# Two transformer blocks on one core: joined slots in the paired-head attention stages, reordered stage ends, a multiplication with a second result, and two weight tiles split early

## The chip, the cores and the metric

The program runs on one core of one Trainium2 chip. The metric is the device time of one execution in microseconds (us), as the median of three runs. The core's engines are TensorE (PE in the profile, PEld for its weight loads), VectorE (DVE), ScalarE (ACT), GpSimd (POOL) and SyncE (SP, which here only issues DMAs). Each works through its own instructions in order and waits on semaphores that the others raise.

## What is computed

Two blocks of two layers each on a sequence of 512 tokens with 1024 features, all in float32. Cut to what matters here:

```python
def first_block(...):                       # two layers
    h = h + even_mixer(...)                 # layer 0: moba attention (8 heads), diff attention (4 x 2 heads)
    h = h + conv_ffn(...)                   # up, 3-tap convolution, gelu, product, down
    h = h + odd_mixer(...)                  # layer 1: dilated attention (8 heads), low-rank attention "mla" (4 heads)
    h = h + conv_ffn(...)
    return rmsnorm(h, final_norm)

def second_block(...):                      # two layers, each:
    ya = global_axial_attention(...)        # 8 query heads
    yb = pool_mixer(...)
    yc = neighbourhood_attention(...)       # 8 heads
    merged = jnp.sum(gates * z, axis=2)     # gated sum of the three branches
    mix = jnp.einsum('bsd,de->bse', merged, w_out[l])
    x = x + rmsnorm_2(mix, norm_mix_post[l])
    f = conv_gated_mlp(rmsnorm_2(x, norm_ffn_pre[l]), ...)
    x = x + rmsnorm_2(f, norm_ffn_post[l])
```

## The kernel before

**Matrices.** Activations lie transposed, 128 features x 512 tokens to a tile. Every float32 operand of a projection is held as a high and a low part (`hh`/`hl`, `yh`/`yl`, `acth`/`actl`, `mh`/`ml` for activations, `wh`/`wl` for weights), and `three` (L513 to L520) makes one product of 128 x 128 by 128 x 512 with three matmuls (L518, L519, L520). Such a trio is called a part below. An output tile of a 1024-deep projection takes eight parts. SP loads weight tiles (entries) into `raw[0]` and `raw[1]` by turns, POOL splits each with a cast (L474) and a subtraction (L476) into slot 0 or 1 of `wh` and `wl`, and may do so only when the product that read that slot before is done (`entry_done`). Results go to the PSUM banks PA, PB, S0, S1, T0, T1, O0, O1.

**Paired-head attention stages** are moba, dil, axial (twice) and na (twice). Each has 32 tiles of scores: four groups g of two heads, each with four query tiles. All engines run over the same slots t (`attention`, one function on each engine):

- PE, at even t: the scores of tiles t and t+1 (S0 and S1, L733; the two heads use 64 rows of the array each). At every t: as many waiting projection parts of the next group as the list `FILL` or the last plan says, then the transposes of tile t-3 (`transposed`, L646, into T0 or T1 by turns). At even t also the products with the values of the tile pair that ends with t-5 (`weighted_pair`, L781).
- DVE, at t: `score` moves the scores out of PSUM with the bias and the row minimum (L1679; axial L1675); at odd t `scale_pair` takes two reciprocals (L1690) and multiplies two tiles of exponentials by them in place (L1693).
- ACT, at t: the exponential of tile t (`soften_here`, L1338), and behind it the copy of the transposes of tile t-3 from T0 or T1 to SBUF (`copy_turned4`, L1343). In axial, ACT has the root for the next queries ahead of the exponential at t%8 = 6 (`q_root`, L1407).

The transposes of tile tt wait for `p_scaled` of tt (DVE) and for the ACT copy of tile tt-2, which held the same bank. The value products wait for the copies of both their tiles. `FILL` is 3, 3, 2, 2, 3, 3, 0, 0 parts for t%8 = 0 to 7 (axial 3, 3, 2, 0, 0, 0, 0, 0, with the rotation of the next queries, `q_turn`, at t%8 = 5). A pair is an even slot and the odd one behind it; the pair at t%8 = 6 has no parts in groups 0 to 2. It is called an empty pair.

**Other stages that the change touches.** diff is an attention stage with the same slots but one map per two tiles; DVE's `take_k` (L1749) frees PB and makes the next keys. mla runs four heads through 16 score tiles. At the ends of blocks `x_add` on DVE (L1927, L1929, L1582) and `renew_out` on ACT (L1287, L1290, L1291) add the residual, split the sum and make squares; with `early=True` (after diff, stage out0) the first four tiles lie in PA, PB, S1 and S0. In the second block out2 (`out_tiles`) is followed by a norm (`stat_last`), and by up2, whose first unit runs gate and value product side by side. `turning` (L571) is filler work on PE.

Of the kernel before, what the change touches and what calls it, by code (L numbers as in the profile page):

```python
# [11 lines left out]
S = 512  # L12
P = 128
# [20 lines left out]
    "na_v": (4, 1024), "na_qk": (6, 1024), "merge": (24, 1536), "out2": (8, 1024), "up2": (44, 1024), "down2": (16, 1536),  # L34
# [148 lines left out]
def build(nc, x_in, weights, consts, cols_in, lam_in, rel_in, rpb_in, strips_rel, strips_na, out):  # L183
    with ExitStack() as ctx:
# [159 lines left out]
        def flat(t):  # L344
# [5 lines left out]
                 (spare[:, :], yl[:, 8:10, :].rearrange("p a n -> p (a n)"))]  # L350

# [109 lines left out]
        def _(pool):  # L461
# [4 lines left out]
            def split(name, b):  # L466
                count, width = SEGMENTS[name]
                with pool.Fori(0, count // 2) as i:
# [31 lines left out]
            for n in SEG1:  # L500
                if n == "diff_v":
                    split_diff_v(here("diff_v"))
                else:
                    split(n, here(PHASE_OF.get(n, n)))
            for layer in range(LAYERS2):
                for n in SEG2:
                    split(n, here(PHASE_OF.get(n, n), layer))
# [3 lines left out]
        def _(pe):  # L511
# [186 lines left out]
            def attention(b, b0, kind, last_parts=(), last_plan=()):  # L698
# [43 lines left out]
                for t in range(end + 1):  # L742
# [6 lines left out]
                    for part in parts[max(sum(slots[:t]), begun):sum(slots[:t + 1])]:  # L749
                        part()  # L750
                    if kind == "diff":
                        if t % 2 == 0 and 0 <= t - 4 < 32:
                            difference_turn(b, (t - 4) // 2)
# [3 lines left out]
                    tt = t - T_BEHIND  # L757
                    if 0 <= tt < 32:
                        if tt < 2:
                            pe.wait_ge(v_copied, 4 * b["v"] - 1 + tt)  # L760
                        pe.wait_ge(p_scaled, b["ps"] + tt + 1)
                        pe.wait_ge(pt_copied, u + tt + 1)
                        transposed(tt, span(tt), maps4).then_inc(pt_ready, 1)
                    tv = t - V_BEHIND
                    if 0 <= tv < 32:
                        g, head = tv // 8, tv % 2
                        if head:
                            if tv == 1:
                                pe.wait_ge(y_split, 2 * b["g"] + 1)
                            if tv % 8 == 1:  # L770
                                pe.wait_ge(o_taken, u + 8 * max(g - 1, 0) + 2)
                            pe.wait_ge(pt_copied, u + tv + 3)
                            weighted_pair(OB[g % 2], tv // 2, span(tv), lambda head, k: values(g, 64 * head, k))
# [111 lines left out]
            def first_head(b):  # L885
# [5 lines left out]
                return [query, lambda: head_query(b, 0, False), lambda: head_key(b, 0), lambda: head_turn(b, 0), lambda: head_values(b, 0)]  # L891

            def mla(b, o):
# [26 lines left out]
                for t in range(16 + 3):  # L920
# [25 lines left out]
                    if 0 <= tv < 16:  # L946
                        if tv % 4 == 0:
# [4 lines left out]
                                 lambda k: head_v[tv // 4 % 2][:, k * P:k * P + P]).then_inc(o_ready, 1)  # L952
                out_part(o, 0, 2, (5, 7))
# [52 lines left out]

            def up(b, squared):
# [6 lines left out]
                if squared:  # L1014
                    pe.wait_ge(pa_taken, b["a"] + 1)
# [190 lines left out]
            def moba_stat():  # L1206
# [23 lines left out]
                      [1, 0, 0, 0, 1, 0, 0, 0, 1, 1, 1])  # L1230
# [4 lines left out]
            for l in range(LAYERS2):  # L1235
# [9 lines left out]
                out_tiles(H("out2", l), lambda k: (mh[:, k, :], ml[:, k, :]), m_split, H("out2", l)["m"], 1)  # L1245
# [9 lines left out]
        def _(act):  # L1255
# [24 lines left out]

            def renew_out(b, gain_at, early=False):

                def both(i, banks):
                    for j, (bank, taken) in enumerate(zip(banks, (pa_taken, pb_taken))):
                        n = 2 * i + j
                        act.wait_ge(xs_ready, b["xs"] + n + 1)
# [1059 lines left out]
```

## Time and profile before

| what | us |
|---|---|
| median of 3 runs | 3023.19 (3022.72 to 3024.15) |
| the profiled execution | 3022.8 |
| its span, first to last instruction | 3021.0 |
| PE busy in the span | 2975.2 |
| POOL busy | 1659.4 |
| DVE busy | 1449.0 |
| ACT busy | 774.2 |

A matmul's row lasts longer than its share of the engine, because matmuls overlap: the distance from one start to the next is what counts. An idle time in brackets behind a row is counted from the modelled end of the instruction before. The PEclk column of a stretch gives the share of TensorE's clock that was granted: 1.00 is 2.4 GHz, and 0.5 is 1.2 GHz.

### The profile page before, as it was taken

To read this page: it belongs to the slowest core of one execution; us is meant where nothing else is said; L and a number is where in the kernel's file an instruction comes from. 1 tells how busy PE (TensorE), PEld (TensorE's weight loads), DVE (VectorE), ACT (ScalarE), POOL (GpSimd) and SP (SyncE) were. 2 spreads that over 40 slices of the span, in tenths; PEclk is the share of its full clock that TensorE was granted. 3 is DMA by queue.
4 is the path that set the end of the run, shared out by engine and by line. 5 is a ranking of instruction groups with operands and counts; after the bars stand their busy time and mean duration, and the time that the engine had idled before them with its cause. 6 is when DMAs were issued, how large, how long until landed. Compare 5 with 4: busy or idle time off the path is not lost.

```text
span 3021.0 us, 41775 instructions
## 1 busy us (share of the span) xinstructions
PE 2975.2 (98%) x14292; PEld 2347.9 (78%) x14292; DVE 1449.0 (48%) x2511; ACT 774.2 (26%) x1419; POOL 1659.4 (55%) x1254
## 2 busy tenths in 40 slices
PE   8999999999999999999999999999999999999999
PEld 6767888887688888777688878888767788778887
DVE  4455444225544442365543476640575544576621
ACT  3343222113432210163411132210262411122200
POOL 4434666664156666533266656667423366556674
PEclk9999999999999999999999999999999999999999
DMA  6352223323122233213222222233114222222232
GB/s 159 103 165 79 97 96 106 104 84 93 34 84 94 95 106 107 90 50 80 68 85 103 84 77 97 94 107 104 64 39 103 65 94 94 84 84 96 94 108 90
DMA packets 99737, 276.53 MB, mean 92 GB/s; under 512 B 38014, under 2 KB 38782, under 8 KB 99634
## 3 DMA queue, kind: packets, MB, share of 16 engines
q1 hardware_dynamic: 97184, 269.03, 27.4%
q10 hardware_dynamic: 2450, 6.13, 1.0%
q8 instruction: 64, 1.05, 0.2%
q14 instruction: 39, 0.32, 0.0%
HBM read 271.39 MB, written 11.54 MB: 94 GB/s over the span
## 4 chain that ended last, share of the span: by engine, by line
PE 94%; DVE 3%; issue 1%; ACT 0%; POOL 0%; DMA 0%; ACTq 0%; DVEq 0%; POOLq 0%
PE PA L518 13%; PE PA L520 12%; PE PA L519 12%; PE PB L518 10%; PE PB L520 10%; PE PB L519 10%; PE S L733 3%; PE O L781 3%; PE T L646 3%; PE O L518 3%; PE O L519 3%; PE O L520 3%; PE O L550 1%; PE S L634 1%; PE S L636 1%
## 5 line engine op out<-in xcount | busy, mean ns | idle before, releaser
L476 POOL TENSOR_TENSOR wl<-raw,wh 128x1024 fp32r<-128x1024 f32 (+3 forms) x410 | 1110.8, 2709 | 32.9
L473 POOL TENSOR_TENSOR zero<-zero 128x1 f32<-128x1 f32 x410 | 82.3, 201 | 1287.5 <-PE PA L520 533.2
L518 PE MATMUL PA<-hh,wh 128*128 128x512 f32 x1152 | 471.3, 409 | 9.0 <-DVE hl L1576 9.0
L474 POOL CAST wh<-raw 128x1024 fp32r<-128x1024 f32 (+3 forms) x410 | 470.2, 1147 | 0.0
L520 PE MATMUL PA<-hh,wl 128*128 128x512 f32 x1152 | 450.9, 391 | 0.0
L519 PE MATMUL PA<-hl,wh 128*128 128x512 f32 x1152 | 450.8, 391 | 0.0
L518 PEld LDWEIGHTS PA<-hh,wh 128*128 128x128 f32 x1152 | 217.2, 189 | 101.4 <-issue 52.8
L518 PE MATMUL PB<-hh,wh 128*128 128x512 f32 x720 | 287.4, 399 | 1.2 <-DVE tmps L1996 1.2
L520 PE MATMUL PB<-hh,wl 128*128 128x512 f32 x720 | 280.9, 390 | 0.0
L519 PE MATMUL PB<-hl,wh 128*128 128x512 f32 x720 | 280.6, 390 | 0.0
L519 PEld LDWEIGHTS PA<-hl,wh 128*128 128x128 f32 x1152 | 217.6, 189 | 46.8 <-issue 5.1
L520 PEld LDWEIGHTS PA<-hh,wl 128*128 128x128 f32 x1152 | 217.3, 189 | 46.8
L1976 DVE SCALAR_TENSOR_TENSOR tmps<-S,cols,tmps 128x511 f32<-128x511 f32 (+1 forms) x264 | 198.0, 750 | 37.6 <-DVE tmps L1976 9.1
L518 PEld LDWEIGHTS PB<-hh,wh 128*128 128x128 f32 x720 | 135.1, 188 | 42.2 <-issue 13.4
L520 PEld LDWEIGHTS PB<-hh,wl 128*128 128x128 f32 x720 | 135.1, 188 | 28.8
L519 PEld LDWEIGHTS PB<-hl,wh 128*128 128x128 f32 x720 | 135.4, 188 | 27.4 <-issue 0.7
L1437 ACT ACTIVATE T<-tmps 128x512 f32<-128x512 f32 x88 | 53.0, 602 | 376.8 <-DVE tmps L1976 376.8
L518 PE MATMUL O<-hh,wh 128*128 128x512 f32 x368 | 143.4, 390 | 2.7 <-POOL wl L476 2.7
L520 PE MATMUL O<-hh,wl 128*128 128x512 f32 x368 | 143.2, 389 | 0.0
L519 PE MATMUL O<-hl,wh 128*128 128x512 f32 x368 | 143.2, 389 | 0.0
L1439 ACT ACTIVATE acth<-T 128x512 f32 x88 | 52.7, 599 | 338.3 <-DVE T L2002 338.3
L518 PE MATMUL PA<-acth,wh 128*128 128x512 f32 x352 | 137.4, 390 | 0.0
(389 smaller groups left out, 5411.7 us busy)
## 6 DMA issues: line engine op xcount, KB each, us to landing
raw<-in_w_up SPq DMA_DIRECT2D x176, 512.0 KB, 3.2
raw<-in_w_down SPq DMA_DIRECT2D x64, 768.0 KB, 4.3
raw<-in_w_merge SPq DMA_DIRECT2D x48, 768.0 KB, 4.3
raw<-in_w_out SPq DMA_DIRECT2D x30, 512.0 KB, 3.2
strips_na<-in_rpb SPq DMA_DIRECT2D x1, 7620.0 KB, 31.4
raw<-in_w_pool SPq DMA_DIRECT2D x12, 512.0 KB, 3.2
raw<-in_w_na_qk SPq DMA_DIRECT2D x12, 512.0 KB, 3.3
raw<-in_w_na_v SPq DMA_DIRECT2D x8, 512.0 KB, 3.2
```

The lines of the kernel that those rows point to most:

```text
L473: nc.gpsimd.tensor_tensor(zero[:, :], zero[:, :], zero[:, :], ALU.add)
L474: nc.gpsimd.tensor_copy(wh[s][:, 0:width], raw[s][:, 0:width]).then_inc(w_head, 1)
L476: nc.gpsimd.tensor_tensor(wl[s][:, 0:width], raw[s][:, 0:width], wh[s][:, 0:width].bitcast(F), ALU.subtract).then_inc(w_split, 1)
L518: mm(dst, h_, rh, start=first, stop=False)
L519: mm(dst, h_, rl, start=False, stop=False)
L520: return mm(dst, l_, rh, start=False, stop=last)
L646: last = nc.tensor.transpose(TB[t % 2][:, k * P:k * P + P], src[t % len(src)][:, k * P:k * P + P], ident[:, :])
L733: mm(SB[head][:, 0:span(t)], queries[g % 2][r, qt * P:qt * P + P], (axial_key if kind == "axial" else keys[g % 2])[r, 0:span(t)], start=Tr ...
L781: last = mm(bank[r, q], values(head, k), turned4[2 * (n % 2) + head][:, k * P:k * P + P], start=(k == 0), stop=(k == L // P - 1))
L1437: A(GELU[:, :], tmp[0][:, :], f).then_inc(gelu_ready, 1)
L1439: A(tile(acth, i), PROD[:, :], ACT.Copy).then_inc(act_hi, 1)
L1976: ins = STT(out=dst[:, lo:hi], in0=src[:, lo - d:hi - d], scalar=w(k), in1=dst[:, lo:hi], op0=ALU.mult, op1=ALU.add)
```

## The change

1. **Joined slots.** In the four kinds of paired stages PE does at even t the scores and the parts of both slots, and at odd t the transposes of tiles t-3 and t-2, and then the value products of the pair t-5, t-4. ACT's and DVE's order in these stages stays as it was.
2. **The multiplication with a second result.** In moba, axial and na, `scale_pair` multiplies with an added minimum over the row, written to an unused column.
3. **diff.** `take_k` stands ahead of the score of its slot, and one remainder (`turned_rest`) is moved.
4. **Stage ends.** `x_add` and `renew_out` with `early` overlap the first four tiles; every `renew_out` and `square_out` begins with a dummy square root.
5. **dil to mla, and mla.** The parts of head 0 of mla come in another order, and DVE and ACT take them one to two slots earlier; in mla the second query product stands behind the value products of its slot, and DVE moves the outputs out before the next score.
6. **Early weight tiles.** The first two entries of up2 travel with out2's entries, as its entries 2 and 5, and POOL splits them into free parts of `actl` and `yl`. up2's first unit reads them there, so that its second unit finds its weights in slots 0 and 1.

```diff
+            def split_out2(b):
+
+                split_one("out2", b, 0, -1)
+                split_one("out2", b, 1, 0)
+                split_one("out2", b, 2, None, first_unit[0])
+                for n, m in ((3, 2), (4, 3)):
+                    split_one("out2", b, n, m - 1, pair(m))
+                split_one("out2", b, 5, None, first_unit[1])
+                for n, m in ((6, 4), (7, 5), (8, 6), (9, 7)):
+                    split_one("out2", b, n, m - 1, pair(m))
...
-                    for part in parts[max(sum(slots[:t]), begun):sum(slots[:t + 1])]:
-                        part()
...
-                    tt = t - T_BEHIND
-                    if 0 <= tt < 32:
...
-                    tv = t - V_BEHIND
...
+                    if t % 2 == 0:
+                        for part in parts[max(sum(slots[:t]), begun):sum(slots[:t + 2])]:
+                            part()
+                        continue
+                    for tt in (t - T_BEHIND, t - T_BEHIND + 1):
+                        if 0 <= tt < 32:
+                            if tt < 2:
+                                pe.wait_ge(v_copied, 4 * b["v"] - 1 + tt)
+                            pe.wait_ge(p_scaled, b["ps"] + tt + 1)
+                            pe.wait_ge(pt_copied, u + tt + 1)
+                            transposed(tt, span(tt), maps4).then_inc(pt_ready, 1)
+                    tv = t - V_BEHIND + 1
...
+                        pe.wait_ge(pt_copied, u + tv + 3)
+                        weighted_pair(OB[g % 2], tv // 2, span(tv), lambda head, k: values(g, 64 * head, k))
...
-                return [query, lambda: head_query(b, 0, False), lambda: head_key(b, 0), lambda: head_turn(b, 0), lambda: head_values(b, 0)]
+                return [query, lambda: head_key(b, 0), lambda: head_query(b, 0, False), lambda: head_turn(b, 0), lambda: head_values(b, 0)]
...
                         if q == 0:
                             head_key(b, h + 1)
-                            head_query(b, h + 1, True)
...
+                    if h < 3 and q == 0:
+                        head_query(b, h + 1, True)
...
-                            last = three(bank[:, :], wsl(s, k), hs(k), k == 0, k == DT - 1)
+                            last = three(bank[:, :], tuple(t[:, k * P:k * P + P] for t in first_unit[s]), hs(k), k == 0, k == DT - 1)
...
-                      [1, 0, 0, 0, 1, 0, 0, 0, 1, 1, 1])
+                      [1, 0, 1, 0, 1, 0, 0, 0, 1, 0, 1])
...
+            def root_table():
+                A(held_act, one[:, :], ACT.Sqrt)
...
                 if early:
-                    both(0, (PA, PB))
-                    both(1, (S1, S0))
+                    head(0, PA)
+                    head(1, PB)
+                    keep(0, 0, PA)
+                    head(2, S1)
+                    keep(0, 1, PB)
+                    head(3, S0)
+                    keep(1, 0, S1)
+                    keep(1, 1, S0)
...
-                    TS(e, e, rden[:, m % 8:m % 8 + 1], None, ALU.mult).then_inc(p_scaled, 1)
+                    if steady:
+                        TS(e, e, rden[:, m % 8:m % 8 + 1], None, ALU.mult, ALU.min,
+                           accum_out=stats[:, 116 + m % 4:117 + m % 4]).then_inc(p_scaled, 1)
+                    else:
+                        TS(e, e, rden[:, m % 8:m % 8 + 1], None, ALU.mult).then_inc(p_scaled, 1)
...
-                    if kind not in ("axial", "diff") and t < 24 and t % 8 == K_AT:
+                    if kind != "axial" and t < 24 and t % 8 == K_AT:
                         take_k(ahead(g), g + 1)
```

How the rows move, at two places. On PE in the first na stage, the end of group 0, from the scores of the empty pair (t = 6) to those of t = 8; S, T and O are PSUM banks, probs, biased, y_tok and probsT hold exponentials and their transposes. Before:

```order
L733 MATMUL S<-k_sb,q_sb 128x512 x2
L646 MATMUL T<-ident,probs 128x128 x4
L781 MATMUL O<-probsT,V 64x128 x8
L646 MATMUL T<-ident,biased 128x128 x4
L733 MATMUL S<-kr_sb,qr_sb 128x512 x2
```

After, where the names of the buffers are one pair further on:

```order
L761 MATMUL S<-kr_sb,qr_sb 128x512 x2
L674 MATMUL T<-ident,biased 128x128 x8
L812 MATMUL O<-y_tok,V 64x128 x8
L761 MATMUL S<-k_sb,q_sb 128x512 x2
```

The second four transposes have moved from behind the value products to directly behind the first four, and both kinds of work are one tile nearer to the scores.

On DVE at the start of out0's `x_add`, where hl is the remainder of the split, and acc the sum of squares. Before:

```order
L1927 TENSOR_TENSOR PA<-x,PA 128x512
L1929 SCALAR_TENSOR_TENSOR hl<-PA,cols,hh 128x512
L1582 TENSOR_TENSOR acc<-acc,tmps 128x512
L1927 TENSOR_TENSOR PB<-x,PB 128x512
L1929 SCALAR_TENSOR_TENSOR hl<-PB,cols,hh 128x512
L1582 TENSOR_TENSOR acc<-acc,tmps 128x512
L1927 TENSOR_TENSOR S<-x,S 128x512
```

After:

```order
L1988 TENSOR_TENSOR PA<-x,PA 128x512
L1988 TENSOR_TENSOR PB<-x,PB 128x512
L1992 SCALAR_TENSOR_TENSOR hl<-PA,cols,hh 128x512
L1988 TENSOR_TENSOR S<-x,S 128x512
L1992 SCALAR_TENSOR_TENSOR hl<-PB,cols,hh 128x512
L1639 TENSOR_TENSOR acc<-acc,tmps 128x512
L1988 TENSOR_TENSOR S<-x,S 128x512
```

The sums of the next tile now stand ahead of the remainder of the one before, which waits for ACT.

## Rows read from the trace of the kernel before

**Rows 1.** The page, part 1: busy time, share and instructions.

```profile
PE 2975.2 (98%) x14292; PEld 2347.9 (78%) x14292; DVE 1449.0 (48%) x2511; ACT 774.2 (26%) x1419; POOL 1659.4 (55%) x1254
```

**Rows 2.** PE's waits: who waited for whom, total us, times, longest.

```profile
PE O L518 <- POOL wl L476: 2.7, 2, 1.3
```

**Rows 3.** Timeline of PE, an empty pair in na: start, us, instruction.

```profile
1483.43 1.13 PE L733 MATMUL S<-k_sb,q_sb 64*128 64x512 f32 x4
1484.49 0.66 PE L646 MATMUL T<-ident,probs 128*128 128x128 f32 x4
1485.08 1.09 PE L781 MATMUL O<-probsT,V 128*64 128x128 f32 x16
1486.69 1.13 PE L733 MATMUL S<-kr_sb,qr_sb 64*128 64x512 f32 x4
```

**Rows 4.** Timeline of na, from scores to exponential, with parts behind them.

```profile
1445.36 1.13 PE L733 MATMUL S<-kr_sb,qr_sb 64*128 64x512 f32 x4
1446.42 0.50 PE L518 MATMUL PA<-hh,wh 128*128 128x512 f32 x1
...
1446.53 0.69 DVE L1679 CUSTOM_DVE_ANT_0 probs<-S,tmps 128x512 f32<-128x512 f32 x1 [2.01 <-issue]
...
1446.76 0.40 PE L519 MATMUL PA<-hl,wh 128*128 128x512 f32 x1
...
1447.26 0.72 ACT L1338 ACTIVATE probs<-probs,stats 128x512 f32<-128x512 f32 x1 [1.19 <-DVE stats L1679]
```

**Rows 5.** Timeline of na, DVE, POOL, PE and ACT around one stretched multiplication.

```profile
1429.67 3.13 DVE L1693 TENSOR_SCALAR biased<-biased,stats 128x512 f32<-128x512 f32 x2
...
1430.10 2.42 POOL L476 TENSOR_TENSOR wl<-raw,wh 128x1024 fp32r<-128x1024 f32 x1
...
1434.16 2.60 PE L733 MATMUL S<-kr_sb,qr_sb 64*128 64x512 f32 x4 [1.70 <-DVE stats L1679]
...
1434.05 0.72 ACT L1338 ACTIVATE probs<-probs,stats 128x512 f32<-128x512 f32 x1 [4.13 <-DVE stats L1679]
...
1434.77 0.57 ACT L1343 ACTIVATE y_tok<-T 128x512 f32<-128x512 f32 x1
```

**Rows 6.** Stretches: length, busy time of PE, PEld, DVE, ACT, POOL, PEclk, DMA.

```profile
1434.60:1441.50 6.90, 6.90 (x17) 4.18 (x15) 1.70 (x8) 2.75 (x8) 0.00 (x0) 0.51 0.84 165
...
2322.10:2325.60 3.50, 3.50 (x9) 2.56 (x9) 1.67 (x6) 1.77 (x5) 0.00 (x0) 0.51 0.97 192
```

**Rows 7.** Timeline of axial, the query rotation on PE and the root on ACT.

```profile
1335.39 1.05 PE L838 MATMUL PB<-onesblk,tmps 128*128 128x2 f32 x8
...
1337.25 0.60 PE L646 MATMUL T<-ident,probs 128*128 128x128 f32 x4
...
1338.99 1.28 ACT L1407 ACT_TABLE_LOAD   x1
...
1341.86 0.72 ACT L1338 ACTIVATE probs<-probs,stats 128x512 f32<-128x512 f32 x1
```

**Rows 8.** Timeline of PE in diff, scores of groups 2 and 3.

```profile
191.16 1.06 PE L733 MATMUL S<-k_sb,q_sb 64*128 64x128 f32 x4 [0.84 <-DVE k_sb L1749]
...
211.17 0.46 PE L733 MATMUL S<-kr_sb,qr_sb 64*128 64x128 f32 x2 [0.85 <-DVE kr_sb L1749]
```

**Rows 9.** Timeline of PE in out0, its seventh tile.

```profile
263.67 0.65 PE L518 MATMUL PA<-yh,wh 128*128 128x512 f32 x1 [2.53 <-ACT x L1291]
```

**Rows 10.** Timeline of PE at the start of the second block's second layer.

```profile
2141.17 0.50 PE L518 MATMUL PA<-hh,wh 128*128 128x512 f32 x1 [1.53 <-DVE hl L1576]
```

**Rows 11.** Groups by line and form in axial's stretch: busy us, mean ns.

```profile
L1675 DVE TENSOR_SCALAR_CACHE_REDUCE biased<-S,stats 128x512 f32<-128x512 f32 x16 | 11.4, 745 | 1.3 <-PE T L646 0.7 <-PE S L733 0.6
```

**Rows 12.** One line's instructions, all of the run: min/median/max ns.

```profile
L1693 DVE TENSOR_SCALAR biased<-biased,stats x96: 274/482/2589, 54.7 to 2385.9; 128x512 f32<-128x512 f32 x64, 128x128 f32<-128x128 f32 x16, 128x384 f32<-128x384 f32 x16
```

**Rows 13.** PE's waits from 700 to 835 us (dil and mla).

```profile
PE O L669 <- ACT probsT L1333: 1.3, 3, 0.7
PE PB L916 <- DVE y_tok L1902: 1.3, 1, 1.3
```

More of the change, by code:

```diff
@@ L464, in _, with split @@
             nc.gpsimd.memset(one[:, :], 1.0).then_inc(w_split, 1)
-            def split(name, b):
+            def split(name, b, first=0):
                 count, width = SEGMENTS[name]
-                with pool.Fori(0, count // 2) as i:
+                with pool.Fori(first, count // 2) as i:
                     for s in range(2):
@@ L504, in _, with pair, split_up2 @@
                     split(n, here(PHASE_OF.get(n, n)))
+            def pair(m):
+                return wh[m % 2][:, 0:1024], wl[m % 2][:, 0:1024]
+            def split_out2(b):
[7 more added lines that the diff above has]
+                    split_one("out2", b, n, m - 1, pair(m))
+            def split_up2(b):
+                split_one("up2", b, 0, -3)
+                split_one("up2", b, 1, -2)
+                split("up2", b, 1)
             for layer in range(LAYERS2):
                 for n in SEG2:
-                    split(n, here(PHASE_OF.get(n, n), layer))
+                    b = here(PHASE_OF.get(n, n), layer)
+                    if n == "out2":
+                        split_out2(b)
+                    elif n == "up2":
+                        split_up2(b)
+                    else:
+                        split(n, b)
         @block.tensor
@@ L748, in attention @@
                         q_turn(axial_turn(b, t // 8 + 1))
-                    for part in parts[max(sum(slots[:t]), begun):sum(slots[:t + 1])]:
-                        part()
                     if kind == "diff":
+                        for part in parts[max(sum(slots[:t]), begun):sum(slots[:t + 1])]:
+                            part()
                         if t % 2 == 0 and 0 <= t - 4 < 32:
@@ L1005, in rest_out, with mixed_tiles @@
                     project(bank[:, :], m % 2, b["e"] + m - 2, rhs=lambda k: (yh[:, k, :], yl[:, k, :])).then_inc(entry_done, 1)
+            def mixed_tiles(b):
+                for i in range(4):
+                    for s, (bank, taken, key) in enumerate(((PA, pa_taken, "a"), (PB, pb_taken, "b"))):
+                        if s == 0:
+                            pe.wait_ge(m_split, b["m"] - 1)
+                        pe.wait_ge(taken, b[key] + i + 1)
+                        project(bank[:, :], s, b["e"] + (0, 1, 3, 4, 6, 7, 8, 9)[2 * i + s], rhs=lambda k: (mh[:, k, :], ml[:, k, :]),
+                                last_of=(m_split, b["m"]) if s == 0 else None).then_inc(entry_done, 1)
             def up(b, squared):
@@ L1790, in attention @@
                         take_q(ahead(g), g + 1)
-                    if kind == "diff" and t < 24 and t % 8 == K_AT:
-                        take_k(ahead(g), g + 1)
                     if gate is not None and t == 35:
@@ L1803, in attention @@
                     if kind != "diff" and t < 32 and head:
[L1804 removed]
+                        scale_pair(u, t, L, kind != "dil")
                     if kind == "diff" and t >= 16 and t % 8 == 0:
                         y_norm(b, t // 8 - 2)
[L1807 to L1811 removed]
+                    if kind == "diff" and t - 2 in Y_TURN[1:]:
+                        turned_rest(b, ytile, Y_TURN.index(t - 2))
                 done((1 if kind == "axial" else 4) * UNIT_LINKS.get(kind, UNIT_LINKS["causal"]))
@@ L1891, in mla @@
                     h, q = t // 4, t % 4
-                    if t < 16:
-                        score(u, t, "mla", (q + 1) * P, causal[:, (3 - q) * P:S])
-                    if 0 <= t - 2 < 16:
-                        invert(u, t - 2)
                     tv = t - 4
@@ L1903, in mla @@
                            ALU.mult).then_inc(o_taken, 1)
+                    if t < 16:
+                        score(u, t, "mla", (q + 1) * P, causal[:, (3 - q) * P:S])
+                    if 0 <= t - 2 < 16:
+                        invert(u, t - 2)
                     if h < 3:
@@ L2294, in weight_streams @@
         per["merge"].append(np.concatenate([gates, br], 3).transpose(1, 0, 2, 3).reshape(24, P, 1536))
-        per["out2"].append(stationary(a["w_out_2"][l]))
+        mixed = stationary(a["w_out_2"][l])
         val, gate, d = feed_forward(a["w_up_2"][l], a["w_down_2"][l])
-        per["up2"].append(interleave(gate, val))
+        units = interleave(gate, val)
+        per["out2"].append(np.concatenate([mixed[:2], units[:1], mixed[2:4], units[1:2], mixed[4:]]))
+        per["up2"].append(units[2:])
         per["down2"].append(d)
```

107 lines of the change are left out of this document (60 added, 47 removed).

## The prediction, made before the changed kernel was run

> **What bounds the kernel now.** First the engines' busy time: PE works 2975.2 of 3021.0 us, the others 26 to 55% [rows 1]. So the time is PE's row of instructions plus its 46 us of waits, and an edit on DVE, ACT, POOL or SP counts only through a wait of PE. The profiled execution took 3022.8 us, 1.8 more than its span and 0.4 under the median, so the sum is made against 3022.8. Then the timelines of the stages that change. A part is three matmuls; with starts 0.23 apart it is 0.69 us. The empty pair of na shows the price of each step: scores 1.06 (1483.43 to 1484.49), four transposes 0.59, then value products and four transposes 1.61 together, so 3.26 for the pair [rows 3]. No wait stands in it. PE has no slack left there, but ACT and DVE have a chain behind each pair of scores that PE now comes nearer to.
>
> **Joined slots, what they bring.** The first matmul of a part behind scores has its successor 0.34 later (1446.42 to 1446.76) where a plain one has 0.23 [rows 4]: 0.11 for starting a row of parts. A filled pair had two such starts, behind the scores and behind the transposes, and keeps one; with the second return from transposes (0.09, the difference between the 0.59 of the first four and some 0.50 of a plain row of four) I take 0.2 a pair. 12 to 13 filled pairs in each of six stages make 75 x 0.2 = -15. The new neighbour, value products straight to scores, is in no row of before. It is bounded by nothing (then another 0.09 to 0.12 a pair, -9 in all, is gained) and by what value products to transposes cost; I take the latter, since both are changes of the array's shape, 64 x 128 against 128 x 64. The Trainium skill (TensorEngine Tiling (Array Packing), Key Properties) says that changing the tiling mode, not only the tile, drains TensorE. By it the change of neighbour saves nothing there; by the low bound the sum would be 9 lower.
>
> **Joined slots, what they cost.** This term decides. In the changed order the second four transposes of the odd slot belong to tile P-1, if P is the even slot whose scores were just made. They need the bank that ACT empties with its copy of tile P-3, and ACT has that copy behind the exponential of tile P, which waits for DVE's score of P, which waits for the very scores that PE has just done. Before, those transposes stood behind the next pair's scores, so the copy had a whole pair more. The length of the chain from the start of the scores: DVE starts 1.17 later (1445.36 to 1446.53), ACT's exponential another 0.73 later (1447.26) and takes 0.72 [rows 4], the copy takes 0.57 [rows 5], and a hand-over of 0.04: 3.23. PE comes to those transposes after scores and the first four, 1.06 + 0.59 = 1.65, plus 0.69 for each part in the pair [rows 3, 4]. So a pair with no part waits 1.58, one with one part 0.9, one with two 0.2, one with three or more nothing. moba, dil and na have three empty pairs each, at t%8 = 6 of groups 0 to 2: 4 stages x 3 x 1.6 = +19. In axial ACT also has the root ahead of that exponential: from the start of its first table load to the end of the exponential pass 3.59 (1338.99 to 1342.58) [rows 7]. Counted from the scores at t = 4: ACT gets the query sums at 1.06 + 1.86 [rows 7], one copy and the copy of the query tile bring it to about 5.0, 3.59 and 0.57 to 9.2; PE has scores, 1.86, transposes and values (2.2), scores and four transposes (1.65), 6.8. So about 2.2 to 2.4, six times: +13. Pairs with one or two parts, in group 3 and beside axial's rotation, are a dozen or so, most with two, and two with none: about +8, the least certain of these. Together the six stages: -15 + 19 + 13 + 8 = **+25**. If ACT's chain is shorter than I have it (the score could start 0.1 earlier, since it needs only the first bank), each empty pair loses 0.1 to 0.3 less: 2 to 5 in all.
>
> **The clock.** Two stretches have half the clock, 1.2 of 2.4 GHz, 6.9 and 3.5 us long [rows 6]; the first begins at 1434.6 behind a PE wait of 1.70 [rows 5], and I find the same after 2.53 at 263.67 [rows 9], while 1.53 at 2141.17 is followed by none [rows 10]. A fall of 3.4 us costs half, 1.7. The new waits of 1.6 lie between 1.53 and 1.70, those of axial above both. I take it that five of the eighteen end in a fall, mostly in axial: **+8.5**. Bounds: none (0) and all (+31).
>
> **The multiplication with a second result.** In na PE waited 1.70 because one pair of multiplications took 3.13 us beside POOL's subtraction of 2.42 [rows 5]; the longest alone was 2.59 and 3.1, the median 0.48 [rows 12]. The same happened in the second layer, with the second fall. The nearest row of a DVE operation of this kind with accumulation, L1675, takes 0.745 and shows nothing stretched in its mean [rows 11], though it reads PSUM. The Trainium skill (SBUF — State Buffer, SBUF: two separate sides) says that DVE in a two-port mode and GpSimd share a port pair, and whoever has it blocks the other for the whole instruction; [rows 5] agree. Whether the accumulation takes the multiplication off that pair, no row shows; I take it, since at 0.745 it is at single rate. Then both waits and their falls go: 2 x 1.70 + 6.8/2 + 3.4/2 = **-8.5**. The added 0.27 us a tile is on DVE, loaded 50 to 70% in these stages: nothing on PE, except 0.27 more on a chain that no rows above contain.
>
> **diff.** Scores of groups 1, 2 and 3 wait 0.84, 0.84 and 0.85 for `take_k` [rows 8]. Ahead of DVE's score it ends about 0.7 earlier, and its price is that the score behind it is 0.7 later, which the exponentials of diff bear. The last wait is followed by a fall of 3.4: 3 x 0.84 + 1.7 = **-4.2**.
>
> **Stage ends.** out0's seventh tile waits 2.53 for ACT's copy in `renew_out` [rows 9]. Interleaved, ACT gets each sum one DVE step earlier, and by the count of its steps the fourth tile's copy is done before PE comes: -2.53 and the fall, -1.7: **-4.2**. The dummy square roots move a table load ahead of a sum; at the other ends PE does filler matmuls meanwhile: 0. Value and gate of up2 wait 1.3 twice for POOL [rows 2]; the early tiles take that away: **-2.7**, if POOL's two extra splits in out2 are hidden, where POOL has 1400 us of idle. The tail of dil and mla: waits of 1.3 and 1.3 [rows 13] for DVE's outputs and ACT's copies, which come one to two slots earlier: **-2.6**.
>
> **The sum.** 3022.8 + 25 + 8.5 - 8.5 - 4.2 - 4.2 - 2.7 - 2.6 = 3034; with the shorter chain 3029 to 3032. I forecast **3031**, from 3026 to 3042.
>
> **The rivals.** 0.2% is 6 us, so 3017.1 and 3029.2 bound "the same"; less than that a measurement of this kernel can hardly tell.
> - The waits come, but at 1.6 and 2.4 us behind small work they bring no falls: 3031 - 8.5 = 3022. For it: 1.53 without a fall [rows 10]. Against: 1.70 with one [rows 5]. 0.25.
> - The waits are much shorter, since ACT comes to the copy first in many pairs, or the values-to-scores change is free: half of the 40 us of waits goes, and with them the falls: 3031 - 20 - 8.5 = 3002, from 2985 to 3015, faster. For it: all other edits gain 22 by rows. Against: ACT's order is written out by hand and has the exponential first. 0.22.
> - Falls at nearly every new wait, slower: decisive if the granted clock drops at 1.6 us of idle. Thirteen more falls x 1.7 = +22: 3053. 0.09.
> - The accumulation doesn't keep DVE from POOL's port. Then the na waits stay: 3031 + 8.5 = 3040. 0.08.
> The forecast itself has 0.36.
>
> **How the numbers follow.** Above 3029.2 are the forecast less a small part, the falls and the port, with a tenth of what is left: 0.51. Within: most of the rival without falls, 0.26. Below 3017.1: the shorter waits and the rest, 0.23. For 8 in 10 the range goes from 3000, which leaves out the lower half of the third case, to 3050, which leaves out the worst of the falls.
>
> **What would show it.** PE's waits for ACT's copies of transposes: today next to none, by the forecast 18 to 30, of 1.5 to 2.4 us, one in every empty pair, which lasts 4.8 instead of 3.26 [rows 3]. If that pair lasts under 3.6, the forecast fails. The multiplication at a constant 0.75 with nothing near 2.6, and no 1.70 in na; a stretched one shows the port rival. 0.84 gone from diff, 2.53 from out0, 1.3 from up2. Where the clock column of the paired stages stays at 1.00, there were no falls. In filled pairs one start of 0.34 where there were two; two would mean that joining brings nothing.

## The result and the profile after

The changed kernel takes 3044.85 us (median of four runs, 3044.20 to 3046.54), the kernel before 3022.95 beside it. The ratio is 1.0071, with a 95% interval of 1.0055 to 1.0087: slower by 21.9 us. The prediction said 3031, range 3000 to 3050, and slower with a chance of 0.51. The direction and the mechanism held; the forecast moved by 8 where 22 came.

The page of the changed kernel, its span and part 1, answers to [rows 1]:

```profile
span 3044.8 us, 41860 instructions
PE 2967.8 (97%) x14292; PEld 2348.3 (77%) x14292; DVE 1428.0 (47%) x2671; ACT 765.8 (25%) x1427; POOL 1659.9 (55%) x1254
```

PE does the same 14292 matmuls in 7.4 us less of busy time [rows 1], and the span is 23.8 longer: 31 us more of waiting. PE's waits over the whole run (who waited for whom, total us, times, longest) say for what:

```profile
PE T L674 <- ACT y_tok L1400: 37.8, 30, 2.6
...
PE T L674 <- ACT probsT L1400: 3.6, 9, 0.9
PE PA L546 <- POOL wl L491: 3.2, 4, 1.2
...
PE S L761 <- DVE stats L1736: 1.4, 4, 0.5
```

The first two rows are new: transposes that wait for ACT's copy of earlier transposes, 39 times and 41.4 us. In before this stood at 0.7 in all. The third was 2.7 in two waits [rows 2]; now four waits lie in out2. The last is the na stall of 1.70 [rows 5] gone, and what remains of diff's.

Here is the empty pair of na after the change, all engines, to lay beside [rows 3]:

```profile
1468.28 1.13 PE L761 MATMUL S<-kr_sb,qr_sb 64*128 64x512 f32 x4
1469.34 0.66 PE L674 MATMUL T<-ident,biased 128*128 128x128 f32 x4
1469.45 0.69 DVE L1736 CUSTOM_DVE_ANT_0 probs<-S,tmps 128x512 f32<-128x512 f32 x1 [1.43 <-issue]
...
1470.18 0.72 ACT L1395 ACTIVATE probs<-probs,stats 128x512 f32<-128x512 f32 x1 [2.17 <-DVE stats L1736]
...
1470.90 0.58 ACT L1400 ACTIVATE y_tok<-T 128x512 f32<-128x512 f32 x1
...
1471.62 0.63 PE L674 MATMUL T<-ident,biased 128*128 128x128 f32 x4 [1.62 <-ACT y_tok L1400]
...
1472.17 1.09 PE L812 MATMUL O<-y_tok,V 128*64 128x128 f32 x16
...
1473.20 1.13 PE L761 MATMUL S<-k_sb,q_sb 64*128 64x512 f32 x4
```

Read it from the last wait back. The transposes at 1471.62 need the bank that the copy at 1470.90 empties. The copy stands behind the exponential at 1470.18. ACT had been idle for 2.17 before that, waiting for DVE's score at 1469.45, which needs the scores that PE began at 1468.28. The copy's own data had been there since the pair before. From scores to scores the pair takes 4.92 us, where it took 3.26 [rows 3]. The chain from 1468.28 to 1471.62 is 3.34.

The clock fell seven times instead of four. Below are two of the stretches at half the clock, in moba and in axial (columns as in [rows 6]), and one at the full clock: it lies behind a wait of 2.56 in axial, up to 2269.97, which no fall followed.

```profile
70.88:74.29 3.41, 3.41 (x9) 2.64 (x9) 1.08 (x8) 0.94 (x4) 0.00 (x0) 0.50 0.78 104
1347.47:1350.88 3.41, 3.41 (x23) 2.10 (x21) 1.59 (x5) 0.68 (x3) 0.00 (x0) 0.50 0.02 5
...
2269.97:2273.40 3.43, 3.43 (x27) 2.22 (x28) 2.27 (x8) 1.04 (x3) 0.00 (x0) 1.00 0.02 5
```

Since PE has the same number of matmuls in every kernel here, the distance between two kernels can be read at any matmul: the start of the n-th in one less that of the n-th in the other. This gives a ledger by stage, in us against the kernel before. The last two columns are of experiments below, by their numbers.

| stage | changed | not joined (experiment 5) | copy first (experiment 2) |
|---|---|---|---|
| moba | +6.2 | 0.0 | -2.8 |
| diff | -2.1 | -2.1 | -2.1 |
| out0 (wait 2.7, fall 1.7) | -4.4 | -4.4 | -4.4 |
| dil | +2.1 | -1.8 | -4.7 |
| mla | -2.4 | -2.4 | -2.4 |
| axial, layers 1 and 2 | +12.5, +10.9 | +1.9, +2.2 | -2.6, -2.5 |
| na, layers 1 and 2 | -1.2, +0.5 | -5.3, -3.6 | -8.1, -6.5 |
| out2, layers 1 and 2 | +2.2, +2.2 | +2.2, +2.2 | +2.2, +2.2 |
| up2, layers 1 and 2 | -1.6, -1.5 | -1.6, -1.5 | -1.6, -1.5 |

Everything else is within 0.1, but for up to 1.2 us at the start of the program, which differ from run to run.

### The profile page after: what moved, and what is told of

It reads as the page before. It is cut to its first block, busy times and chain, and to the rows that moved or that the text cites. A ratio compares the mean times of both kernels' runs of the same rounds, so it can differ in the third digit from the quotient of the medians.

```text
span 3044.8 us, 41860 instructions
## 1 busy us (share of the span) xinstructions
PE 2967.8 (97%) x14292; PEld 2348.3 (77%) x14292; DVE 1428.0 (47%) x2671; ACT 765.8 (25%) x1427; POOL 1659.9 (55%) x1254
## 4 chain that ended last, share of the span: by engine, by line
PE 88%; issue 4%; DVE 4%; ACT 3%; POOL 1%; DMA 0%; ACTq 0%; DVEq 0%; POOLq 0%
PE PA L546 12%; PE PA L547 12%; PE PA L548 12%; PE PB L546 10%; PE PB L548 10%; PE PB L547 10%; PE O L548 3%; PE O L547 3%; PE O L546 3%; PE O L812 2%; PE S L761 2%; PE T L674 2%; PE O L578 1%; PE S L662 1%; PE S L664 1%
## 5 line engine op out<-in xcount | busy, mean ns | idle before, releaser
L478 POOL TENSOR_TENSOR wl<-raw,wh 128x1024 fp32r<-128x1024 f32 (+3 forms) x386 | 1049.1, 2718 | 31.0
L475 POOL TENSOR_TENSOR zero<-zero 128x1 f32<-128x1 f32 x386 | 76.2, 197 | 1279.5 <-PE PA L548 517.5
L546 PE MATMUL PA<-hh,wh 128*128 128x512 f32 x1136 | 457.2, 402 | 6.0 <-DVE hl L1633 6.0
L476 POOL CAST wh<-raw 128x1024 fp32r<-128x1024 f32 (+3 forms) x386 | 445.0, 1153 | 0.0
L546 PE MATMUL PB<-hh,wh 128*128 128x512 f32 x704 | 278.8, 396 | 1.2 <-DVE tmps L2074 1.2
L548 PE MATMUL PB<-hh,wl 128*128 128x512 f32 x704 | 274.5, 390 | 0.0
L547 PE MATMUL PB<-hl,wh 128*128 128x512 f32 x704 | 274.2, 390 | 0.0
```

What stands on the lines that cost most here:

```text
L475: nc.gpsimd.tensor_tensor(zero[:, :], zero[:, :], zero[:, :], ALU.add)
L476: nc.gpsimd.tensor_copy(wh[s][:, 0:width], raw[s][:, 0:width]).then_inc(w_head, 1)
L478: nc.gpsimd.tensor_tensor(wl[s][:, 0:width], raw[s][:, 0:width], wh[s][:, 0:width].bitcast(F), ALU.subtract).then_inc(w_split, 1)
L546: mm(dst, h_, rh, start=first, stop=False)
L547: mm(dst, h_, rl, start=False, stop=False)
L548: return mm(dst, l_, rh, start=False, stop=last)
```

## The experiments

All times are medians but for the last experiment's, which is one execution; before took 3022.5 to 3023.3 beside them.

**1. The joined slots alone.** The kernel before, with only this on TensorE (the parts of both slots at even t, both transposes and the value products at odd t):

```diff
-                    for part in parts[max(sum(slots[:t]), begun):sum(slots[:t + 1])]:
...
+                    if t % 2 == 0:
+                        for part in parts[max(sum(slots[:t]), begun):sum(slots[:t + 2])]:
...
+                    for tt in (t - T_BEHIND, t - T_BEHIND + 1):
...
```

> The kernel before with TensorE's joined slots alone, ACT's and DVE's orders as before. Theory (ACT's copy stands behind the exponential of the scores just made): the 39 waits of the changed kernel, 41.4 us, appear here too, with some seven falls of the clock of 1.7 us each, against some 11 us saved by fewer changes of work: 3023 + 41.4 + 12 - 11 = 3065 us, empty pairs 4.8 us in na. Rival (the loss comes from the slower multiplication on the chain of DVE): the copy waits are small here, under 10 us in all, and the time is 3010 to 3025.

It took 3084.0 us, ratio 1.0208 (1.0192 to 1.0223): +61 us. The waits for ACT's copy are there, as the theory has it, but are larger than in the changed kernel, and the longest is 4.7:

```profile
PE T L646 <- ACT y_tok L1346: 53.6, 31, 4.7
...
PE T L646 <- ACT probsT L1346: 5.5, 11, 0.9
```

The rival (it is the slower multiplication) falls, since it isn't in this kernel. It is 19 us worse than my 3065. The waits in na are the reason: 3.17, 3.17 and 4.67 in each layer, where the changed kernel has 1.62. The third experiment shows where they come from.

**2. The copy ahead of the exponential.** The changed kernel with one edit on ScalarE, for even slots of the joined stages:

```diff
+                    tt = t - T_BEHIND
+                    if kind != "diff" and t % 2 == 0 and 0 <= tt < 32:
+                        copy_turned4(u, tt, S if full else (tt // 2 % 4 + 1) * P)
                     if kind == "axial" and t < 24 and t % 8 == TURN["root"]:
                         q_root(axial_turn(b, t // 8 + 1)["r"])
...
-                    if kind != "diff" and 0 <= tt < 32:
+                    if kind != "diff" and t % 2 and 0 <= tt < 32:
                         copy_turned4(u, tt, S if full else (tt // 2 % 4 + 1) * P)
```

> The changed kernel with one edit on ACT: in the even slots of the joined stages the copy of the transposes stands ahead of the exponential (and of axial's root) instead of behind it. Theory: the waits for that copy (41.4 us) and the falls of the clock that follow them (7 x 1.7 = 12 us) go, and nothing takes their place, since ACT is idle there: 3045 - 53 = 2992 us, 2990 to 3000. Rival (the chain through DVE and the bank is as long in any order): at most half goes, 3015 to 3030.

It took 2988.51 us, ratio 0.9888 (0.9873 to 0.9903): 56 us less than the changed kernel, 34 less than before. The same empty pair, all engines:

```profile
1435.41 0.60 ACT L1400 ACTIVATE y_tok<-T 128x512 f32<-128x512 f32 x1
...
1435.79 1.13 PE L761 MATMUL S<-kr_sb,qr_sb 64*128 64x512 f32 x4
1436.85 1.09 PE L674 MATMUL T<-ident,biased 128*128 128x128 f32 x8
...
1437.69 0.72 ACT L1395 ACTIVATE probs<-probs,stats 128x512 f32<-128x512 f32 x1 [1.68 <-DVE stats L1738]
1437.87 1.09 PE L812 MATMUL O<-y_tok,V 128*64 128x128 f32 x16
...
1438.90 0.70 PE L761 MATMUL S<-k_sb,q_sb 64*128 64x512 f32 x2
```

The copy starts at 1435.41, before the scores do, and ends at 1436.01, 0.84 before the first of the transposes. The eight transposes run in a row, and the pair takes 3.11 us, less than the 3.26 of before and 1.81 less than in the changed kernel. Only two waits for a copy are left, 0.5 us in all, and the clock doesn't fall at all before the program's last microsecond. So the whole loss of the change is one position in ACT's order. Of the 56 us, 7 falls x 1.7 = 12 are the clock's by my price for a fall, and 44 the waits', which sum to 41.4 in the trace.

**3. The multiplication as before.** The changed kernel with `scale_pair` never steady:

```diff
-                        scale_pair(u, t, L, kind != "dil")
+                        scale_pair(u, t, L, False)
```

> The changed kernel with the multiplication as it was before (no second result), nothing else undone. Theory (the second result takes DVE off the way that it shares with POOL): multiplications of 2.6 us come back beside POOL's subtraction, and na waits 1.7 us more in each layer, with one or two falls of the clock: 3045 + 3.4 + 3.4 = 3052 us. Rival (the stall of before went by the new order alone, POOL and DVE no longer meeting there): 3045 us, or less, if the 0.27 us of the slower form is on the path.

It took 3070.05 us, ratio 1.016 (1.0145 to 1.0176): 25 us more than the changed kernel, where I expected 7. The last empty pair of na in layer 1:

```profile
1500.83 4.06 DVE L1754 TENSOR_SCALAR biased<-biased,stats 128x512 f32<-128x512 f32 x2
...
1501.12 3.48 POOL L478 TENSOR_TENSOR wl<-raw,wh 128x1536 fp32r<-128x1536 f32 x1
...
1505.41 0.68 DVE L1736 CUSTOM_DVE_ANT_0 probs<-S,strip 128x512 f32<-128x512 f32 x1
...
1506.14 0.72 ACT L1395 ACTIVATE probs<-probs,stats 128x512 f32<-128x512 f32 x1 [4.57 <-DVE stats L1736]
...
1506.86 0.57 ACT L1400 ACTIVATE y_tok<-T 128x512 f32<-128x512 f32 x1
...
1507.58 1.08 PE L674 MATMUL T<-ident,biased 128*128 128x128 f32 x4 [4.67 <-ACT y_tok L1400]
```

POOL subtracts on a 1536 wide weight for 3.48 us, DVE's two multiplications take 4.06 instead of about 0.9, and the score, the exponential and the copy all stand behind them. A stall of DVE that cost before only what was over PE's slack (one 1.70 in each na stage) is now added in full to a chain on which PE waits anyway: 3.17, 3.17 and 4.67 where the changed kernel has 1.62. At each of these six waits the clock falls, in the wait or within 0.3 us behind it. The two stages are 12.7 and 12.6 us longer than in the changed kernel: 6.2 in each are the longer waits, and the rest goes with the falls. The form with a second result is steady, beside POOL too. The changed kernel's multiplication by line and form (min/median/max ns), to compare with [rows 12]:

```profile
L1751 DVE TENSOR_SCALAR_CACHE_REDUCE biased<-biased,stats x80: 342/743/748, 55.2 to 2410.1; 128x512 f32<-128x512 f32 x64, 128x128 f32<-128x128 f32 x8, 128x384 f32<-128x384 f32 x8
...
L1751 DVE TENSOR_SCALAR_CACHE_REDUCE probs<-probs,stats x80: 474/744/748, 59.4 to 2415.0; 128x512 f32<-128x512 f32 x72, 128x256 f32<-128x256 f32 x8
```

The longest of 160 is 0.748, where 2.59 stood [rows 12], and 3.11 in the other half of the instructions before:

```profile
L1693 DVE TENSOR_SCALAR probs<-probs,stats x96: 339/485/3114, 58.9 to 2390.6; 128x512 f32<-128x512 f32 x80, 128x256 f32<-128x256 f32 x16
```

It is not that they no longer meet. In the changed kernel 38 of the 160 run beside one of POOL's subtractions and none lasts over 0.748; in the kernel before 34 of 192 do, and 24 of these take over 0.8.

**4. The early weight tiles alone.** The kernel before with the `first_unit` places, the order of out2's entries and up2's first unit:

```diff
-                out_tiles(H("out2", l), lambda k: (mh[:, k, :], ml[:, k, :]), m_split, H("out2", l)["m"], 1)
+                mixed_tiles(H("out2", l))
...
-                            last = three(bank[:, :], wsl(s, k), hs(k), k == 0, k == DT - 1)
+                            last = three(bank[:, :], tuple(t[:, k * P:k * P + P] for t in first_unit[s]), hs(k), k == 0, k == DT - 1)
```

> The kernel before with the early weight tiles of up2 alone. By the trace of the changed kernel out2 waits for POOL 1.2 and 0.4 us in each layer and loses 2.2, and up2 gains 1.6: 3023 + 1.3 = 3024.3 us. Rival (what out2 loses belongs to another part of the change): up2's gain alone, 3023 - 3.1 = 3019.8 us.

It took 3021.96 us, ratio 1.0000 (0.9991 to 1.0009): its time can't tell +1.3 from nothing, and excludes the rival's -3.1 only just. The positions can: +2.21 in out2 and -1.58 in up2 in layer 1, +2.2 and -1.6 in layer 2. The -3.1 us by which na came out shorter in this run is a matter of the clock (one fall of 3.4 there where the profile of before had 6.8 and 3.4), and hides the loss. POOL in out2, this kernel, shows where the 2.2 is from:

```profile
1704.86 0.65 POOL L488 TENSOR_TENSOR zero<-zero 128x1 f32<-128x1 f32 x1
1705.44 1.04 POOL L489 CAST actl<-raw 128x1024 fp32r<-128x1024 f32 x1
1706.56 2.40 POOL L491 TENSOR_TENSOR actl<-raw,actl 128x1024 fp32r<-128x1024 f32 x1
1708.92 0.64 POOL L488 TENSOR_TENSOR zero<-zero 128x1 f32<-128x1 f32 x1
1709.50 1.03 POOL L489 CAST wh<-raw 128x1024 fp32r<-128x1024 f32 x1
```

An extra split lasts 4.06 us (1704.86 to 1708.92). In the steady pace of out2 in the kernel before, POOL idles 1.79 a tile:

```profile
1723.30 0.20 POOL L473 TENSOR_TENSOR zero<-zero 128x1 f32<-128x1 f32 x1 [1.79 <-PE PB L520]
```

The split of the next tile begins at 1708.92, where it was 1706.95 before, and this kernel had been 0.4 ahead: 2.4 later, and PE waits for it.

**5. Everything but the joined slots.** The changed kernel with TensorE's order of before in the paired stages (the reverse of the first diff).

> The changed kernel with TensorE's order in the paired stages put back to that before (every other part of the change kept). Theory: the other parts together gain, by the positions read so far: out0 and diff 6.5, mla 2.4, na's stall and falls 7 to 8.5, against the early weight tiles' 1.3: 3022.9 - 15 to 17 = about 3007 us, and no wait for ACT's copies. So joining alone costs 38 us here, and beside the copy-first order (2988.5) it would gain 18. Rival (the loss is in the other parts too): over 3015 us.

It took 3009.2 us, ratio 0.9951 (0.9934 to 0.9967), 2 us over the expectation. Two kernels differ only in joining with a good order on ACT on one side: 3009.2 - 2988.5 = 20.7 us is what joining is worth when nothing waits, 2.8 to 3.0 us in each of moba, dil, na and na, 4.5 and 4.7 in axial. (The copy first without joining was not run; since PE's waits for these copies come to 0.2 us without joining, I give that order no share.) The extra of 1.9 in axial is a wait that I had not expected in the unjoined order. PE's waits there, from 1300 to 1400 us:

```profile
PE S L761 <- DVE probs L1729: 0.9, 3, 0.6
PE PB L866 <- ACT tmps L1448: 0.3, 1, 0.3
```

In before this window has no wait. The slower multiplication makes DVE late for axial's scores. The listed waits are 1.2 of the 1.9 us; the rest lies in delays of axial's score matmuls too short for the list.

**6. The second result alone.** The kernel before with `scale_pair` of the changed kernel.

> The kernel before with the second result of the multiplication alone. Theory: the two na waits of 1.7 us and the falls of the clock behind them (3.4 and 1.7) go, and nothing else moves: 3022.9 - 8.5 = 3014.4 us; the multiplication takes 0.75 us everywhere, beside POOL too. Rival (the slower form, 0.27 us more a tile, costs in the unjoined order as much as the stall): 3020 to 3026 us.

It took 3018.51 us, ratio 0.9983 (0.9974 to 0.9993): -4.8 against the 3023.3 beside it, little over half the expectation. By positions na gains 5.3 and 3.6, as expected, and axial loses 1.9 and 1.9 (with the waits just shown), which the theory left out.

**7. Copy first, with the plain multiplication.** The second kernel with the edit of the third.

> The kernel with the copy ahead of the exponential (2988.5 us), with the multiplication as it was before. Theory: the stretched multiplications of 2.5 to 3.6 us come back and delay the scores' release, but with no copy behind the exponential PE waits only for what is over its slack: some 1.5 to 3 us in each of six empty pairs of na, and falls: 3000 to 3012 us. Rival (it was the copy's chain alone that made the stall hurt; in the kernel with plain order it cost 25 us): under 2992 us, little or nothing.

It took 2996.22 us, ratio 0.9908 (0.9891 to 0.9924): 7.7 over the second kernel, a little under the range. The stall is there, and PE meets it at its source instead of behind the copy, with one wait of 2.04 and one fall in each na stage:

```profile
PE T L674 <- DVE biased L1756: 6.1, 7, 2.0
```

So the multiplication's form is worth 25 us in the changed kernel's order, 7.7 in the good one and 4.8 in that of before. The last of these is a balance: by positions in na alone the stall costs 25.3 us in the changed kernel's order, 9.6 in the good one and 8.9 in that of before, where the slower form costs 3.8 in axial. It is the chain through the copy that makes the stall dear.

**8. The early tiles in other places.** The second kernel, with the first extra tile ahead of out2's entries, and the second behind them:

```diff
-                split_one("out2", b, 0, -1)
-                split_one("out2", b, 1, 0)
-                split_one("out2", b, 2, None, first_unit[0])
...
+                split_one("out2", b, 0, None, first_unit[0])
+                for m in range(8):
+                    split_one("out2", b, m + 1, m - 1, pair(m))
+                split_one("out2", b, 9, None, first_unit[1])
...
```

> The kernel with the copy ahead of the exponential, and the two early weight tiles of up2 in other places: the first ahead of all of out2's entries, where POOL idles 4.2 us, the second behind them all, where PE does the norm. Theory (an extra split of 4.0 us does not fit into the 1.8 us that POOL idles in each tile of out2): out2's loss of 2.2 us in each layer goes, and up2 keeps its gain: 2988.5 - 4.4 = 2984.1 us. Rival (the second tile comes too late for the first unit, which starts 7 us after out2's end): it only moves the wait, 2986 to 2989 us.

It took 2984.22 us, ratio 0.9868 (0.9852 to 0.9885), the fastest here, 39 us under before. POOL splits the first extra tile at 1663.72, where it idled 3.05 us in the second kernel. The split takes 3.62 here, so the next tile begins 0.5 later, and the idle time behind it (3.67, where it was 4.20) takes that up. The wait of PE for POOL is gone from the whole list:

```profile
1663.72 0.19 POOL L488 TENSOR_TENSOR zero<-zero 128x1 f32<-128x1 f32 x1
1663.85 1.04 POOL L489 CAST actl<-raw 128x1024 fp32r<-128x1024 f32 x1
1664.97 2.40 POOL L491 TENSOR_TENSOR actl<-raw,actl 128x1024 fp32r<-128x1024 f32 x1
1667.34 0.19 POOL L488 TENSOR_TENSOR zero<-zero 128x1 f32<-128x1 f32 x1
...
1674.98 0.19 POOL L488 TENSOR_TENSOR zero<-zero 128x1 f32<-128x1 f32 x1 [3.67 <-PE PB L544]
```

In this kernel the clock fell once, in diff, behind waits of PE of 0.29, 0.27 and 0.27 us (up to 206.81, 208.09 and 209.29). The second kernel has the same waits there and no fall:

```profile
209.84:213.25 3.41, 3.41 (x12) 2.07 (x10) 2.61 (x12) 3.37 (x10) 0.00 (x0) 0.50 0.99 295
```

**9. diff, the stage ends and mla alone.** The kernel before without any edit to the paired stages, the multiplication or up2.

> The kernel before with the parts that touch neither the paired stages' order, nor the multiplication, nor up2's weights: take_k's place in diff, the overlapped first tiles in out0, the dummy roots, the order from dil to mla. Theory (by the positions in the changed kernel: diff 2.1, out0 2.7 and the fall behind it 1.7, dil's tail 1.8, mla 2.4): 3022.9 - 10.7 = 3012 us. Rival (the prediction's terms for these, 4.2 + 4.2 + 2.6 = 11.0, with diff's fall of the clock worth its 1.7 us): the same sum, but diff alone gains 4.2; the positions in the trace tell them apart, and the time falls to 3010.

It took 3012.66 us (3009.56 to 3014.85), ratio 0.9968 (0.9957 to 0.9980). The positions: diff -2.0, out0 -2.7 and -1.7, dil -1.5, mla -2.5, together -10.4. The time can't tell the two readings of diff apart; the position can, and it is 2.0.

**10. The changed kernel once more**, not altered.

> The changed kernel once more, not altered. Its first profile had waits of 1.52 us at three empty pairs of moba and a fall of the clock behind two of them, none behind na's six waits of 1.6. Theory (whether a fall comes depends on where the wait lies in time by a microsecond or so, not on the wait alone): the same waits to 0.05 us, but another set of falls, 4 to 9 of them, and a time within 4 us of 3045. Rival (each wait of its kind has or has not its fall): the same seven falls at the same places.

It took 3044.29 us (one execution). The waits repeat (37.7 in 30 and 3.6 in 9), the falls do not: six, of which axial has four and moba none. The other two are in dil and in na, at pairs that had none in the first profile:

```profile
734.26:737.67 3.41, 3.41 (x12) 2.52 (x11) 1.60 (x10) 1.25 (x5) 0.00 (x0) 0.50 0.57 186
1495.43:1498.84 3.41, 3.41 (x20) 1.72 (x16) 1.42 (x4) 0.28 (x1) 0.00 (x0) 0.50 0.70 228
```

The rival falls. A wait of 1.5 to 2.6 us may be followed by a fall or not; that it is the wait's place in time that decides was not shown, only that its length alone does not. The two profiles also price a fall, since the kernel is the same: moba is 3.1 us longer with two falls than with none, dil and na 1.6 each with one more, axial in layer 2 1.5. So a fall costs 1.5 to 1.6 us, a little under the 1.7 that I count.

## Why the prediction was right, and where its sizes were off

The step on which it rested held to a tenth: "They need the bank that ACT empties with its copy of tile P-3, and ACT has that copy behind the exponential of tile P". The pair was forecast at 4.84 and lasts 4.92; the six waits of na are 1.62 where 1.58 stood, axial's long ones 2.07 and 2.56 where "2.2 to 2.4" stood. The one edit of experiment 2 takes all but 0.5 us of it away, which shows the cause. By kind, the 41.4 us are 18.9 in the twelve empty pairs of moba, dil and na (19 predicted), 14.4 in the six of axial (13) and 8.1 in the other 21 (8). The terms, with what they measured:

| term | predicted | measured | from |
|---|---|---|---|
| waits for the copies | +40 | +44 | experiment 2 against changed, less the falls |
| new falls of the clock | +8.5 (5) | +12 (7) | profile of changed |
| joining, when nothing waits | -15 | -20.7 | experiment 5 against 2 |
| second result | -8.5 | -4.8 | experiment 5 in na and axial |
| diff | -4.2 | -2.1 | positions |
| out0 | -4.2 | -4.4 | positions |
| early weight tiles | -2.7 | +1.3 | positions, experiment 4 |
| dil's tail, mla | -2.6 | -4.2 | positions |

The measured column makes +21, the time +21.9. The predicted terms made +11, and I named 8, taking 3 off for a shorter chain that was not there (3.34 against the 3.23 of the sum). The direction owes something to luck: with 0.51 for slower it was hardly more than an even bet, and the time lies 5 us under the upper bound. The waits and the falls cost more than forecast, and the gains of diff, the second result and the early tiles were taken too high; joining and dil's end with mla gained more than forecast, which made up for part of it.

- **Early weight tiles: the wrong sign.** The step that failed is "if POOL's two extra splits in out2 are hidden, where POOL has 1400 us of idle". That idle time is a sum over the run. In the stretch that counts POOL idles 1.79 a tile, and the split takes 4.06. Experiment 8 puts the same splits where the stretch has room, and the 2.2 us of each layer are gone.
- **diff: half.** Two errors of size. The three waits of 0.84 became 0.29 and did not vanish: behind `take_k` PE waits for the score that this one pushed back ("which the exponentials of diff bear"). And the fall at 212.67 was worth nothing. In the profile of experiment 6, with the same order in diff as before, it didn't come, and diff took as long (to 0.05 us): PE then waited 0.96 for DVE just behind, so the slow matmuls had filled a wait.
- **Second result: half.** "nothing on PE, except 0.27 more on a chain that no rows above contain" was that chain: in axial, without joining, it costs 1.9 us a layer (experiments 5 and 6). In na alone the gain was 8.9, as forecast. That the form is not stretched beside POOL came out as taken: the longest is 0.748.
- **Joining: a quarter too small.** 0.2 us a pair was near: 2.85 us in a stage, over its 16 pairs, is 0.18, and the empty pairs gain too (3.11 in experiment 2 against 3.26), which the prediction put at nothing. What I missed besides is that in axial joining also takes away the wait just named: 4.6 instead of 2.9. The new neighbour at its full price was right: value products to scores take 1.03 (1472.17 to 1473.20), value products to transposes took 1.02.
- **dil's tail and mla: too small, and from other waits.** Of the two waits in [rows 13] the one for DVE's outputs went. The one for ACT's copies did not: it is 1.6 in the changed kernel. The gain came from waits that the prediction left out: 1.2 and 0.3 for DVE at the end of dil, which are gone, and 1.20 inside mla, put down to nothing that the profile shows, now 0.42. The first line is of the kernel before, the second of the changed one:

```profile
PE PB L872 <- DVE mix L1873: 1.2, 1, 1.2
...
PE O L697 <- ACT probsT L1390: 1.6, 3, 0.7
```

- **The falls.** Five of eighteen was a guess; seven came in the first profile and six in the second. At the 1.5 to 1.6 us that experiment 10 gives for one, the seven are 11 us and not 12, and the waits 45. Since the same wait has one or has none, only a number of them can be forecast, and not their places.

Of the rivals, that of the shorter waits fell (39 waits, 41.4 us), and that of POOL's port too. The one without falls and the one with a fall at each wait bounded what came: 7, of the 18 waits that the prediction counted.

## What to carry to other kernels

When work of one engine is pulled together, go through the orders of the other engines for what it now needs earlier: a result whose input is old can stand behind an instruction that waits for the newest input, and moving that one copy was worth 56 us here, where the change without it lost 22. Price an extra piece of work on an idle engine by the idle time between two deadlines in the stretch where it lands (1.79 us here), not by its idle time in the run. And what a stall costs is not its own: the stretched multiplications cost na 8.9, 9.6 or 25.3 us, as the chain behind them had slack or not.

## What the runs showed of the hardware

- The multiplication on DVE takes 0.48 us and up to 3.67 beside POOL's subtraction; with an accumulated second result it takes 0.743 with a maximum of 0.748 over 160 instructions, though POOL subtracts beside 38 of them, as beside 34 of 192 in the kernel before. For a chain with little slack the slower form is the faster. The Trainium skill (SBUF — State Buffer, SBUF: two separate sides) says that a DVE operation in a two-port mode and a GpSimd operation lock each other out of a shared port pair for a whole instruction. The stretched rows agree (3.13 us beside 2.42, 4.06 beside 3.48); of the form with a second result the rows show only that it is not held up.
- A fall of TensorE's clock to 1.2 GHz for 3.41 us costs 1.5 to 1.6 us where PE is the bound (experiment 10), and 0 where a wait for another engine stands right behind it (212.67 in the profile of before).
- Falls came behind waits of 1.52 (moba, 70.88) and did not behind waits of 2.56 (axial, 2269.97), and in two profiles of one kernel they came behind different waits of the same length. In the kernel before the wait of 2.53 in out0 had one; in experiment 6 the same wait, 2.50 there, had none. Short waits are no safeguard: experiment 2, with no wait over 1.1 us in its attention stages, had no fall, and experiment 8, with the same waits in diff, had one behind waits of 0.27 to 0.29.
